# FFN up projection with the weight blocks stationary and both halves of the activations as one moving operand

## What is computed

```python
D_MODEL, SEQ, DEPTH = 2048, 256, 2
D_FF = 4 * D_MODEL

def rms_norm(x, g):
    y = x * lax.rsqrt(jnp.mean(x * x, axis=-1, keepdims=True) + EPS)
    return y * g

# in each layer, after the attention/pooling part has been added to x:
f = jnp.square(jax.nn.relu(rms_norm(x, g_ffn_pre) @ w_up)) @ w_down
x = x + rms_norm(f, g_ffn_post)
```

## Time and profile before

| | value |
|---|---|
| median of three runs | 2071.33 us |
| the profiled execution | 2071.96 us |
| its span, first to last instruction | 2070.0 us |
| TensorE matmuls (PE) | 2044.3 us busy, 99% |
| TensorE weight loads (PEld) | 1692.8 us busy, 82% |
| VectorE (DVE) | 1085.2 us, 52% |
| ScalarE (ACT) | 1011.9 us, 49% |
| GpSimd (POOL) | 156.0 us, 8% |
| read from HBM | 378.59 MB, 184 GB/s |

### The profile page before, as it was taken

How to read it: one execution, slowest core, us unless ns; L and a number is a source line. 1 busy time by engine, 2 the same in 40 slices (tenths; PEclk the granted TensorE clock), 3 DMA queues, 4 the chain that set the end, 5 groups by cost and what they waited for, 6 DMA issues and landing times.

```text
span 2070.0 us, 27915 instructions
## 1 busy us (share of the span) xinstructions
PE 2044.3 (99%) x9298; PEld 1692.8 (82%) x9298; DVE 1085.2 (52%) x1196; ACT 1011.9 (49%) x1342; POOL 156.0 (8%) x216
## 2 busy tenths in 40 slices
PE   8999999999999999999999999999999999999998
PEld 6888887888888888888878888878888888888886
DVE  5544657554554554554564456664554554454454
ACT  6444656544543553454464456474444444544542
POOL 1941010000000000000100010200000000000001
PEclk9999999999999999999999999999999999999999
DMA  7664355555655655655466543555466465456453
GB/s 253 205 209 136 123 183 163 197 202 170 197 194 177 198 194 176 218 194 177 162 220 210 169 153 123 177 182 197 168 203 199 163 209 196 162 200 226 162 190 135
DMA packets 196508, 381.53 MB, mean 184 GB/s; under 512 B 11904, under 2 KB 14048, under 8 KB 195808
## 3 DMA queue, kind: packets, MB, share of 16 engines
q1 hardware_dynamic: 196256, 380.19, 54.9%
q10 hardware_dynamic: 192, 0.54, 0.1%
HBM read 378.59 MB, written 2.10 MB: 184 GB/s over the span
## 4 chain that ended last, share of the span: by engine, by line
PE 93%; DVE 2%; DMA 2%; ACT 2%; issue 1%; POOL 0%; DVEq 0%; ACTq 0%; SPq 0%; POOLq 0%
PE acc_bank L392 29%; PE acc_bank L394 29%; PE acc_bank L393 29%; PE t_bank L661 1%; DMA raw<-in_w_in 1%; DVE w_lo L996 1%; PE s_bank L541 1%; PE s_bank L500 1%; PE o_bank L570 1%; DMA raw<-in_w_up 1%; ACT h_hi L721 1%; ACT w_hi L715 1%; PE s_bank L394 1%; PE s_bank L393 1%; PE s_bank L392 1%
## 5 line engine op out<-in xcount | busy, mean ns | idle before, releaser
L996 DVE TENSOR_TENSOR w_lo<-raw,w_hi 128x1024 fp32r<-128x1024 f32 x704 | 862.6, 1237 | 548.8 <-ACT w_hi L715 513.7
L715 ACT CAST w_hi<-raw 128x1024 fp32r<-128x1024 f32 x704 | 734.9, 1053 | 463.7 <-PE acc_bank L394 267.8
L392 PE MATMUL acc_bank<-w_hi,h_hi 128*128 128x512 f32 x1536 | 609.1, 397 | 4.4 <-DVE w_lo L996 3.8
L394 PE MATMUL acc_bank<-w_hi,h_lo 128*128 128x512 f32 x1536 | 600.4, 391 | 0.0
L393 PE MATMUL acc_bank<-w_lo,h_hi 128*128 128x512 f32 x1536 | 599.7, 390 | 0.0
L392 PE MATMUL acc_bank<-w_hi,f_hi 128*128 128x512 f32 x1216 | 477.2, 392 | 0.0
L394 PE MATMUL acc_bank<-w_hi,f_lo 128*128 128x512 f32 x1216 | 473.5, 389 | 0.0
L393 PE MATMUL acc_bank<-w_lo,f_hi 128*128 128x512 f32 x1216 | 473.2, 389 | 0.0
L392 PEld LDWEIGHTS acc_bank<-w_hi,h_hi 128*128 128x128 f32 x1536 | 289.7, 189 | 65.4 <-issue 3.9
L394 PEld LDWEIGHTS acc_bank<-w_hi,h_lo 128*128 128x128 f32 x1536 | 289.2, 188 | 61.5
L393 PEld LDWEIGHTS acc_bank<-w_lo,h_hi 128*128 128x128 f32 x1536 | 289.7, 189 | 57.9
(11 more groups left out here) (149 smaller groups left out, 817.5 us busy)
## 6 DMA issues: line engine op xcount, KB each, us to landing
raw<-in_w_up SPq DMA_DIRECT2D x256, 512.0 KB, 4.6
raw<-in_w_down SPq DMA_DIRECT2D x256, 512.0 KB, 4.9
raw<-in_w_in SPq DMA_DIRECT2D x128, 512.0 KB, 4.9
raw<-in_w_out SPq DMA_DIRECT2D x64, 512.0 KB, 5.0
w_pool_s<-in_w_pool SPq DMA_DIRECT2D x2, 1024.0 KB, 8.8
post_row<-in_g_mix_post SPq DMA_DIRECT2D x2, 1024.0 KB, 7.9
post_row<-in_g_ffn_post SPq DMA_DIRECT2D x2, 1024.0 KB, 8.5
out<-x SPq DMA_DIRECT2D x8, 256.0 KB, 2.2
```

The costliest lines, as they stand in the source:

```text
L392: pe.matmul(bank[:, :], xh, wh, start=begin and k == 0, stop=False)
L394: mm = pe.matmul(bank[:, :], xl, wh, start=False, stop=end and k == 1)
L715: act.copy(w_hi[:, half * PAIRS + p, :], raw[:, p, :]).then_inc(hi_made, 1)
L996: dve.tensor_tensor(w_lo[:, slot, :], raw[:, p, :], w_hi[:, slot, :].bitcast(F32), ALU.subtract).then_inc(lo_made, 1)
```

## The change

Each layer's first up unit stays as it was, and so do all other projections. In the other 15 up units of a layer the roles are swapped: a 128x128 block of `w_hi` or `w_lo` is stationary, and the activations move. `h_hi` and `h_lo` now lie side by side (`h_both`), so that `w_hi` meets both in one matmul of 512 columns, and `w_lo` meets `h_hi` in one of 256. The result has the 512 output columns as four blocks on the partitions, positions along the free axis: the layout that the down units want, with no turn. Two such blocks (`m`) stand in a pair of PSUM banks (`acc_pair[b]`), and VectorE adds the two halves of each (a reduction over 2), then takes ReLU and square in one instruction. ScalarE only rounds to `f_hi`. As positions are no longer on the partitions, the factor 1/rms is taken out of the ReLU, and its square (1/mean square, exponent -1 in place of -0.5) multiplies the down results in `down_sum`. In the first unit, the turn of tile 1 now stands before (0, 3) of the second unit and no longer before (1, 2).

```diff
-    h_hi = at("h_hi", [P, KT, SEQ], F32R, r_h)
-    h_lo = at("h_lo", [P, KT, SEQ], F32R, r_h + 4 * KT * SEQ)
+    h_both = at("h_both", [P, KT, 2, SEQ], F32R, r_h)
+    h_hi, h_lo = h_both[:, :, 0, :], h_both[:, :, 1, :]
...
+    acc_pair = [nc.alloc_psum_tensor(f"acc_pair{t}", [P, 2, CH], F32) for t in range(T)]
+    acc_bank = [pair[:, 0, :] for pair in acc_pair]
+    s_bank = [pair[:, 1, :] for pair in acc_pair]
...
# TensorE
+            def turned_unit(hu, result, before=None):
+                for n in range(4):
+                    b, half = n // 2, n % 2
+                    for p in range(PAIRS):
+                        if before is not None:
+                            before(n, p)
+                        slot = half * PAIRS + p
+                        begin, end = half == 0 and p == 0, half == 1 and p == PAIRS - 1
+                        if begin:
+                            pe.wait_ge(acc_free[b], result + 1)
+                        if b == 0:
+                            pe.wait_ge(lo_made, (hu + half) * PAIRS + p + 1 + RAW)
+                        for m in range(2):
+                            both = acc_pair[b][:, m, :]
+                            high = acc_pair[b][:, m, 0:SEQ]
+                            for k in range(2):
+                                kt = 8 * half + 2 * p + k
+                                col = k * CH + (2 * b + m) * P
+                                wh = w_hi[:, slot, col:col + P]
+                                wl = w_lo[:, slot, col:col + P]
+                                xs = h_both[:, kt, :, :].rearrange("p s n -> p (s n)")
+                                xh = h_both[:, kt, 0, :]
+                                if end and k == 1:
+                                    pe.matmul(high, wl, xh, start=False, stop=False)
+                                    mm = pe.matmul(both, wh, xs, start=False, stop=True)
+                                else:
+                                    pe.matmul(both, wh, xs, start=begin and k == 0, stop=False)
+                                    mm = pe.matmul(high, wl, xh, start=False, stop=False)
+                        if b == 1:
+                            mm.then_inc(w_used, 1)
+                        elif end:
+                            mm.then_inc(acc_done, 1)
...
+                        unit(hu, r, h_hi, h_lo, up_first)
+                        def up_second(n, p):
+                            if (n, p) == (0, 3):
+                                turn_f(1)
+                        turned_unit(hu + 2, r + 1, up_second)
+                    with pe.Fori(2 if first else 0, CHUNKS) as u:
+                        turned_unit(hu + u * 2, r + u)
                     def down_first(n, p):
-                        if (n, p) == (1, 2):
-                            turn_f(g, CHUNKS - 1, 1)
-                        if p == 0:
-                            pe.wait_ge(flo_made, T + l * 32 + g * 8 + (3, 7, 4, 8)[n])
+                        if (n, p) == (0, 0):
+                            pe.wait_ge(flo_made, l * 32 + g * 8 + 4)
+                        if n == 1:
+                            pe.wait_ge(flo_made, l * 32 + g * 8 + 4 + p + 1)
# ScalarE
+                def turned_hi(g, u, b):
+                    act.wait_ge(f_ready, l * 32 + g * 8 + u * 2 + b + 1)
+                    act.copy(f_part(f_hi, u, b),
+                             act_f[:, b, :].rearrange("p (k n) -> p k n", k=2)
+                             ).then_inc(fhi_made, 1)
+                def turned_unit(g, u, hu):
+                    turned_hi(g, u, 0)
                     split_hi(hu + 2, 0)
-                    f_chunk_hi(g, u, 0)
-                    split_hi(hu + 3, 1, (0, 1, 2))
-                    activate(g, u, 1)
-                    split_hi(hu + 3, 1, (3,))
-                    f_chunk_hi(g, u, 1)
+                    split_hi(hu + 3, 1)
+                    turned_hi(g, u, 1)
# VectorE
+                def turned_square(g, u, b):
+                    result_stands(dve, b, a0 + ACC_F + g * 8 + u,
+                                  hu0 + HU_F + g * HU_GROUP + u * 2 + 1)
+                    z = act_f[:, b, :].rearrange("p (k n) -> p k n", k=2)
+                    dve.tensor_reduce(z, acc_pair[b][:, :, :].rearrange("p k (s n) -> p k n s", s=2),
+                                      AX.X, ALU.add).then_inc(acc_free[b], 1)
+                    dve.wait_ge(acc_free[b], 1 + a0 + ACC_F + g * 8 + u + 1)
+                    dve.scalar_tensor_tensor(z, z, 0.0, z, ALU.max, ALU.mult
+                                             ).then_inc(f_ready, 1)
+                def turned_lo(g, u, b):
+                    dve.wait_ge(fhi_made, l * 32 + g * 8 + u * 2 + b + 1)
+                    dve.tensor_tensor(f_part(f_lo, u, b),
+                                      act_f[:, b, :].rearrange("p (k n) -> p k n", k=2),
+                                      f_part(f_hi, u, b).bitcast(F32), ALU.subtract
+                                      ).then_inc(flo_made, 1)
...
+                    def turned_unit(u):
+                        turned_square(g, u, 0)
+                        split_lo(hu + u * 2 + 2, 0, (0,))
+                        turned_lo(g, u, 0)
+                        split_lo(hu + u * 2 + 2, 0, (1, 2, 3))
+                        split_lo(hu + u * 2 + 3, 1, (0, 1, 2))
+                        turned_square(g, u, 1)
+                        split_lo(hu + u * 2 + 3, 1, (3,))
+                        turned_lo(g, u, 1)
...
                     if first:
-                        dve.tensor_copy(dst, acc_bank[t][:, :]).then_inc(acc_free[t], 1)
+                        dve.tensor_scalar(dst, acc_bank[t][:, :], over_mean, None, ALU.mult
+                                          ).then_inc(acc_free[t], 1)
                     else:
-                        dve.tensor_tensor(dst, acc_bank[t][:, :], dst, ALU.add
-                                          ).then_inc(acc_free[t], 1)
+                        dve.scalar_tensor_tensor(dst, acc_bank[t][:, :], over_mean, dst,
+                                                 ALU.mult, ALU.add).then_inc(acc_free[t], 1)
```

More of the change, by code:

```diff
@@ L84 @@
 TB_F = 18
-TB_LAYER = TB_F + FF_GROUPS * CHUNKS
+TB_LAYER = TB_F + 1
 XG_Y = 0
@@ L212, in build @@
     minus_half = own("minus_half", [P, 2])
+    minus_one = own("minus_one", [P, 1])
     ones = own("ones", [P, 1])
@@ L277, in f_out, with f_part @@
         return dst[:, ld(u * 4, 4), h_cols(t)]
+    def f_part(dst, u, b):
+        return dst[:, ld(u * 4 + 2 * b, 2), :]
     def h_pair(l, h, i):
@@ L667, in group, with up_first @@
                     r = a0 + ACC_F + g * (2 * CHUNKS)
-                    h_before = h_first_unit(l, 1) if first else None
-                    def up_first(n, p):
-                        if h_before is not None:
+                    if first:
+                        h_before = h_first_unit(l, 1)
+                        def up_first(n, p):
                             h_before(n, p)
[L673 to L677, removed]
-                            if (n, p) == (1, 2):
-                                turn_f(g, u - 1, 1)
-                            if (n, p) == (3, 2):
-                                turn_f(g, u, 0)
-                        unit(hu + u * 2, r + u, h_hi, h_lo, up_next)
+                            if (n, p) == (3, 2):
+                                turn_f(0)
+                        unit(hu, r, h_hi, h_lo, up_first)
[5 more added lines that the diff above has]
+                        turned_unit(hu + u * 2, r + u)
                     def down_first(n, p):
-                        if (n, p) == (1, 2):
-                            turn_f(g, CHUNKS - 1, 1)
-                        if p == 0:
-                            pe.wait_ge(flo_made, T + l * 32 + g * 8 + (3, 7, 4, 8)[n])
+                        if (n, p) == (0, 0):
+                            pe.wait_ge(flo_made, l * 32 + g * 8 + 4)
+                        if n == 1:
+                            pe.wait_ge(flo_made, l * 32 + g * 8 + 4 + p + 1)
                     def down_last(n, p):
@@ L922, in _, with activate, f_chunk_hi @@
                 mix_square(1, 3)
[L925 to L931, removed]
+                def activate(t):
+                    result_stands(act, t, a0 + ACC_F, hu0 + HU_F + 1)
+                    act.activation(act_f[:, t, :], acc_bank[t][:, :], ACT.Relu
                                    ).then_inc(acc_free[t], 1)
-                    act.wait_ge(acc_free[t], 1 + a0 + ACC_F + g * 8 + u + 1)
+                    act.wait_ge(acc_free[t], 1 + a0 + ACC_F + 1)
                     act.activation(act_f[:, t, :], act_f[:, t, :], ACT.Square
                                    ).then_inc(f_ready, 1)
-                def f_chunk_hi(g, u, t):
-                    act.wait_ge(tb_done[t], l * TB_LAYER + TB_F + g * 4 + u + 1)
-                    act.copy(f_out(f_hi, u, t), t_bank[t][:, :].rearrange("p (k n) -> p k n", k=4)
+                def f_chunk_hi(t):
```

(31 more changed lines are left out.)

37 lines of the change are left out of this document (17 added, 20 removed).

## The result

The changed kernel takes 2076.42 us (median of 13 runs, 2073.77 to 2079.99) against 2071.78 us for the kernel before beside it. The ratio of the two is 1.0026, 95% interval [1.0019, 1.0033]: slower by 0.26%, where 0.5% faster was forecast. The profiled execution took 2075.9 us, with a span of 2074.2.

The account below looks back on a forecast made before the run. TensorE was taken to bound the kernel: 2071.96 - 29.1 (turns) + 7.0 (matmuls) + 7.1 (moved turn) + 3.4 (clock) = 2060.4, stated as 2060 us, 0.5% faster. Its own range was 2053 to 2067, for 8 in 10 2050 to 2081.

Parts of the forecast that it names:

- the sum: Whole kernel: 2071.96 - 29.1 + 7.0 + 7.1 + 3.4 = 2060.4 us, stated as 2060, 0.5% faster; chance 0.50.
- What bounds it: Whole kernel: TensorE, busy 99% of the span, so time is what its instructions take from start to start.
- Turns that go: 30 changed up units: two turns each vanish from TensorE's path, 60 x 0.485 = 29.1 us saved.
- Matmuls: Changed up units: a wide-narrow pair takes 343.7 ns, adding 7 us for 30 units, between 0 and 12.8.
- two readings of a uniform stream: Narrow matmul in changed units: 113.3 ns by proportion or 120 ns with a fixed cost; middle taken, 117 ns.
- 'fixed': Narrow matmul in changed units: the 13.3 ns over columns is a cost per matmul, so 106.7 + 13.3 = 120 ns.
- Rival 2: Changed units: wide matmuls behind narrow ones cost 8 ns more, narrow ones 120 ns; 2081 us, 0.5% slower; chance 0.18.
- Weight loads: Changed units: a load can repeat every 111 ns, so it fits under a 113 to 120 ns narrow matmul, without reserve.
- The moved turn: Second up unit of each layer: TensorE idles 3.57 and 4.36 us for ScalarE's square of tile 1; net +7.1 us.
- The clock: Behind the moved turn's two waits: granted clock falls, losing 1.7 us each, 3.4 us counted; the other end is 0.
- VectorE and the seams: First down unit of each group: VectorE's `f_lo` is ready with 2.1 us reserve, so nothing was counted.

Follow-up runs that it names:

- turns_twice: The kernel before with each of the 64 turns of `act_f` done twice in a row (eight transposes in place of four): 2099.88 us, ratio 1.014.
- t12_all256: The changed kernel with the moved turn put back and nearly every 512-column product split into two of 256: 2074.88 us, ratio 1.0016.
- old_cut_128: The kernel before with the third product of each block cut to 128 of 512 columns in 24 up units, leaving three quarters of it out: 1989.63 us.
- turn_12: The changed kernel with the moved turn of tile 1 put back before (1, 2) of the second unit: 2066.62 us, ratio 0.9972 to the kernel before.
- lo_right: The changed kernel with the 256-column product added to the right half of the PSUM bank in place of the left: 2079.79 us.
- wwnn: The changed kernel with matmuls ordered wide, wide, narrow, narrow in place of wide, narrow, wide, narrow: 2068.99 us, ratio 0.9989 to the kernel before.

## Why the prediction was wrong

The measured 2076.4 us lies inside the range for 8 in 10 (2050 to 2081), but 16.4 us above the sum, outside the forecast's own range (2053 to 2067), and on the slower side.

- **What bounds it:** right. TensorE is at 98%, and times followed its steps to 4 us in every run.
- **Turns that go:** 29.1 us, right. The slope of turns_twice is 0.432 of the 0.485 us per turn, and the down units, which lost one turn and nothing else, took 0.50 us less.
- **Matmuls: the step that failed.** The step is the price of a pair, 343.7 ns, which the sum has as +7.0 us, with 0 to 12.8 as its bounds. Measured: 353.3 ns. 1920 x 353.3 ns - 2880 x 226.7 ns = 678.3 - 652.8 = +25.5 us, 18.5 more than the sum had. The narrow step came out at 117 ns as I had it, but by luck: 117 was the middle of two readings of a uniform stream, and in one it is 120.0. The bounds were wrong as they held the wide step at the 226.7 ns of a stream that has only wide ones. The two ends I weighed were both about a uniform stream, where 'fixed' is true (120.0). Neither says what a mixed one costs, and the trace did show it: the steps of 233 ns behind a turn in the earlier trace rows. (One reading of mine was loose besides: the eight plain float32 matmuls of the earlier trace rows are eight records of four matmuls of the program. The 216 ns per record stand.)
- **Rival 2** had this as 8 ns more for each wide matmul and the narrow at 120, a pair of 355 and 2081 us; measured are 353.3 and 2076.4. It had the right place and nearly the right size, and I gave it 0.18. My reason against it was that steps return to 226.7 after a dozen wide matmuls. The new stream never has a dozen: a narrow one stands in every pair.
- **Weight loads:** hidden, as said: narrow matmuls alone step by 120.0 ns (t12_all256), over the 111 of a load. With 128 columns the cover goes: three matmuls of old_cut_128 take 577 ns, where columns and 13.3 ns each would make 520.
- **The moved turn:** 3.4 + 3.9 us of waits against 3.6 + 4.4 forecast, and turn_12 gets 9.8 us back where I had 7.1 + 3.4 = 10.5. Right.
- **The clock:** fell behind both waits, as said, and so it did in lo_right and wwnn, which have the same two waits. A fall that the kernel before has at 1353 us (mean clock 0.66 in 1353 to 1357) is gone after the change, and another one came, at the start of layer 1. These are the two stretches of the changed kernel:

```profile
1049.00:1053.00 4.00, 4.00 (x15) 3.09 (x14) 3.14 (x7) 3.73 (x14) 0.54 (x1) 0.60 0.79 215
1353.00:1357.00 4.00, 2.30 (x13) 1.86 (x14) 4.00 (x4) 3.73 (x13) 1.08 (x1) 1.00 0.47 144
```

  Both stretches stand behind a wait for x. The length of such a wait does not tell whether a fall follows. Here is first the wait of the kernel before that had one (2.51 us), then the two of the changed kernel, of which the shorter (1.98 us) had one and the longer (2.93 us) had none:

```profile
1351.68 1.78 PE L420 MATMUL t_bank<-ident,x 128*128 128x128 f32 x8 [2.51 <-DVE x L1023]
...
1048.66 1.40 PE L463 MATMUL t_bank<-ident,x 128*128 128x128 f32 x8 [1.98 <-DVE x L1073]
...
1354.69 1.32 PE L463 MATMUL t_bank<-ident,x 128*128 128x128 f32 x8 [2.93 <-DVE x L1073]
```

  In all, the clock fell twice in the kernel before and four times in the changed one. The 3.4 us for two more falls fit, in part because these two exchanged places.

- **VectorE and the seams:** right. The last `f_lo` of the fourth group of layer 0 is ready at 957.25 + 0.68 = 957.9, TensorE needs it at 950.05 + 7 x 1.36 = 959.6: a reserve of 1.6 us, and no wait for `f_lo` shows:

```profile
950.05 0.39 PE L398 MATMUL acc_pair<-w_hi,f_hi 128*128 128x512 f32 x1
...
957.25 0.68 DVE L1336 TENSOR_TENSOR f_lo<-act_f,f_hi 128x512 f32 x1
```

- **The sum with the measured step:** 2071.96 - 29.1 + 25.5 + 7.1 + 3.4 = 2078.9 against 2075.9 in the profiled execution. The stages say where the 3.0 us are, up to 0.2 us that lie outside the span. The layers' first groups rose by 7.9 us where the terms make 9.8 (six changed units at -0.12 each, 7.1 and 3.4): the waits were 0.6 us shorter, and the fall at 1353, 1.7 us, was gone. The six other groups won 0.4 us more than the 2.9 that the terms give their 24 units. The rest is 0.4 us shorter: mainly, the projections up to 209 us took 1.4 us less (two waits for `w_lo`, 0.8 us, did not occur), and the stage with the new fall 0.8 more.

The change alone is then: turns -29.1, spacing +25.5, so a gain of 3.6 us by this account; and the place of one turn, which made a loss of it. The six groups' -3.4 us, for 24 of the 30 units, bear the gain out, and so does turn_12, 5.3 us under the kernel before beside it (its profiled execution has one fall of the clock, that of the kernel before two).

**What stays open** is why a mix of widths costs more than its parts. Shown is that it is not the roles, not the layout, not the bank's columns, not the load's reserve, and not the work of VectorE or ScalarE beside it. It depends on the order and not in one direction: 3.3, 1.0 and 2.0 ns per matmul for ones, twos and fours. In all three the wide ones step by 232 to 236 ns on the mean and the narrow ones by 116 to 119, and the starts repeat in patterns of a few steps. What makes these, no run here shows.

## What to carry to other kernels

When TensorE is the bound, a regrouping with the same number of columns costs what its matmuls cost beyond their columns: here 13.3 ns for each fp32r one, and 1 to 4 ns per matmul more once widths are mixed. Price the new stream from a stretch of the trace that is already mixed, not from a uniform one, and try the order of widths: two by two was 7 to 9 us better than one by one. And check each wait that moves with a piece of code: a turn brought forward by three pieces cost as much (9.8 us) as the removal of 20 turns brought.

## What the runs showed of the hardware

- fp32r matmuls step by columns at 2.4 GHz plus 13.3 ns, in streams of 512 (226.7) and of 256 columns (120.0). In the plain float32 chain each matmul of the program stands in the trace as two records of 256 columns (64 for 32 at L541), and records step by 216 ns, only 2 to 3 over the 213 of 512 columns at 2.4 GHz. By the Trainium skill ("TensorE: Matmul & The Clock Gate", section "Back-to-back issue gap") the fixed part is 2.5 ns. The float32 chain agrees; fp32r does not.
- Streams of mixed widths have a surplus of 1.0 to 4.4 ns per fp32r matmul over that, which depends on the order (the table above).
- A 128-column transpose steps by 108 ns in the stream, while its record is 272 ns long; 27.7 us for 256 more of them in turns_twice.
- Behind waits of TensorE of 3.4 and 3.9 us the granted clock was half for 3.4 us, which costs another 1.7 us; with these two waits gone (turn_12), it stayed full there. Behind waits of 2.0 to 2.9 us for x it fell in some places and not in others.
